# Attention values as one 128-column stationary operand: two passes in place of three, halves added after the product

## The reference, cut to what matters

```
p  = softmax(where(valid, q·k * 64**-0.5 + bias, NEG))      # A, band of 8 chunks
o  = p · v                                                   # einsum 'bhqk,bkhd->bqhd'
mo = softmax(mq · mk * 64**-0.5) · mv                        # M, 4 heads of 64
y  = concat(o, mo) * silu(gate);   x = x + y @ w_out
```

## Time and profile before

| what | value |
|---|---|
| median of three runs | 3016.96 us (3013.03 to 3020.06) |
| span of the profiled execution, first to last instruction | 3014.2 us |
| PE busy | 2789.5 us, 93% |
| PE weight loads busy | 2612.1 us, 87% |
| VectorE busy | 1302.0 us, 43% |
| ScalarE busy | 1317.1 us, 44% |
| GpSimd busy | 684.1 us, 23% |
| mean granted TensorE clock | 0.955 |

### The profile page before, as it was taken

How to read it: one execution, slowest core, us unless ns; L and a number is a source line. 1 busy time by engine, 2 the same in 40 slices (tenths; PEclk the granted TensorE clock), 3 DMA queues, 4 the chain that set the end, 5 groups by cost and what they waited for, 6 DMA issues and landing times.

```text
span 3014.2 us, 46630 instructions
## 1 busy us (share of the span) xinstructions
PE 2789.5 (93%) x18936; PEld 2612.1 (87%) x18936; DVE 1302.0 (43%) x3216; ACT 1317.1 (44%) x2826; POOL 684.1 (23%) x384
## 2 busy tenths in 40 slices
PE   7989999989989999989997988888899989999987
PEld 6979999979989999979987877777699979999887
DVE  4045555552235556652225244444523055555542
ACT  4244544433244555542333355555523245444431
POOL 0212222215121212206211132222142212221212
PEclk9989999999989999989997999999999989999998
DMA  4111111133111112123111000000042111111121
GB/s 148 50 32 56 59 51 48 53 117 99 51 46 50 61 50 71 50 116 100 64 43 32 34 12 10 10 10 3 29 172 73 43 35 64 45 59 45 42 79 65
DMA packets 58197, 171.59 MB, mean 57 GB/s; under 512 B 6720, under 2 KB 15040, under 8 KB 57472
## 3 DMA queue, kind: packets, MB, share of 16 engines
q1 hardware_dynamic: 57984, 168.62, 16.4%
HBM read 134.67 MB, written 33.92 MB: 56 GB/s over the span
## 4 chain that ended last, share of the span: by engine, by line
PE 80%; ACT 9%; DVE 7%; issue 3%; DMA 0%; POOL 0%; SPq 0%; DVEq 0%; ACTq 0%
PE acc L1666 37%; PE acc L1745 10%; PE acc L1618 9%; PE scores L1690 8%; PE turned L1704 6%; PE scores L1576 4%; ACT prob L1147 4%; DVE prob L1407 3%; PE turned L1576 2%; PE scores L1554 1%; DVE pt_split L1436 1%; ACT pt_split L1159 1%; DVE y_sb L1463 1%; ACT prob L1150 1%; PE turned L1716 1%
## 5 line engine op out<-in xcount | busy, mean ns | idle before, releaser
L1666 PE MATMUL acc<-h_split,w_hi 128*128 128x352 f32 (+2 forms) x4860 | 893.2, 330 | 34.1 <-ACT raw L1019 15.3
L1666 PEld LDWEIGHTS acc<-h_split,w_hi 128*128 128x128 f32 x4860 | 790.4, 191 | 62.7 <-ACT raw L1019 19.0
L1490 POOL TENSOR_TENSOR w_lo<-w_raw,w_hi 128x1024 fp32r<-128x1024 f32 (+2 forms) x154 | 333.5, 2168 | 1810.4 <-ACT w_hi L1055 1810.4
L1407 DVE CUSTOM_DVE_ANT_0 prob<-scores,bias 128x256 f32<-128x256 f32 (+9 forms) x576 | 337.6, 633 | 504.7 <-PE scores L1690 501.0
L1436 DVE TENSOR_TENSOR pt_split<-turned,pt_split 128x512 fp32r<-128x512 f32 (+4 forms) x564 | 303.2, 552 | 553.1 <-ACT pt_split L1159 552.6
L1745 PE MATMUL acc<-pt_split,v_split 128*64 128x256 f32 (+6 forms) x3486 | 503.0, 281 | 22.9 <-ACT pt_split L1159 7.3
L1666 PE MATMUL acc<-h_split,w_lo 128*128 128x352 f32 (+2 forms) x2430 | 452.5, 323 | 0.0
L1147 ACT ACTIVATE prob<-prob,stat 128x256 f32<-128x256 f32 (+9 forms) x468 | 303.6, 650 | 329.3 <-DVE stat L1407 329.3
L1745 PEld LDWEIGHTS acc<-pt_split,v_split 128*64 128x64 f32 (+2 forms) x3486 | 405.2, 161 | 40.5 <-issue 14.7
L1666 PEld LDWEIGHTS acc<-h_split,w_lo 128*128 128x128 f32 x2430 | 400.3, 189 | 0.0
L1704 PE MATMUL turned<-ident,prob 128*128 128x128 f32 (+2 forms) x1866 | 290.9, 280 | 96.7 <-DVE prob L1423 51.8
(11 more groups left out here) (129 smaller groups left out, 2785.0 us busy)
## 6 DMA issues: line engine op xcount, KB each, us to landing
w_raw<-w SPq DMA_DIRECT2D x132, 512.0 KB, 3.7
x_scr<-y_sb SPq DMA_DIRECT2D x24, 528.0 KB, 5.5
y_sb<-x_scr SPq DMA_DIRECT2D x24, 528.0 KB, 8.0
y_sb<-x_in SPq DMA_DIRECT2D x16, 528.0 KB, 10.9
mw_raw<-w SPq DMA_DIRECT2D x16, 512.0 KB, 7.6
bias<-rel_in SPq DMA_DIRECT2D x24, 320.0 KB, 4.1
raw<-kcache SPq DMA_DIRECT2D x18, 256.0 KB, 4.0
v_cache<-vcache SPq DMA_DIRECT2D x18, 256.0 KB, 4.0
```

The lines of the kernel that those rows point to most:

```text
L1407: dve.tensor_tensor_reduce(out=prob[0:tile.rows, at:at + tile.width], in0=s_ps[lane][0:tile.rows, tile.at:tile.at + tile.width], in1=bias[ ...
L1490: pool.tensor_tensor(w_lo[:, n % 2, 0:wide], w_raw[:, n % 2, 0:wide], w_hi[:, n % 2, 0:wide].bitcast(F32), ALU.subtract).then_inc(wlo_made ...
L1666: ins = pe.matmul(acc[s.bank][:, 0:s.cols], w[ws][:, 128 * k:128 * k + 128], x(xs, k), start=k == 0 and y == 0, stop=k == s.k_tiles - 1 an ...
```

## The change

For A and M, the values of one block and lane are laid out as four quarters of 64 columns: high of lane 0, low of lane 0, low of lane 1, high of lane 1. The stationary operand is the 128 columns of a lane, high and low together, and there are two passes, with the high and the low half of the probabilities; the low pass waits for `turned_lo` as before, but it now stands behind the first of two passes. For lane 0 the product with the high values is on rows 0 to 63 of `acc[0]` and that with the low values on rows 64 to 127; for lane 1 it is the other way round.

The evacuation becomes: ScalarE copies the rows with the low products into a new SBUF tile `o_low` (two copies of 64 rows, lying where `recip` is), VectorE adds the other rows of `acc[0]` to it (two instructions), waits for that, and multiplies the whole 128 rows into the gate (one instruction, whose end is `o_read`). `acc[0]` is free after the additions (`o_added`). Kinds B and C keep their passes. GpSimd's writing of the ones moves from the start of layer 2 to behind its last M unit.

```diff
+    o_low = sbuf("o_low", [256], at=place[0] - 1024)
+    v_quarters = v_flat[:, 13 * 128:].rearrange("p (b q d) -> p b q d", q=4, d=64)
...
+        if kind == "C":
+            return v_hi[0:rows, block:block + n, :, 0:64], v_lo[0:rows, block:block + n]
+        return v_quarters[0:rows, block:block + n, 0:4:3], v_quarters[0:rows, block:block + n, 1:3]
...
+            elif name == "evac" and item[1].job.kind in "AM":
+                u = item[1]
+                act.wait_ge(*pv_done.upto(u.chunks[-1].p))
+                if u.before is not None:
+                    act.wait_ge(*o_read.upto(u.before.n))
+                act.activation(o_low[0:64, 0:u.qn], acc[0][64:128, 0:u.qn], ACT.Copy).then_inc(o_low_read.mark(u.n), 1)
+                act.activation(o_low[64:128, 0:u.qn], acc[0][0:64, 256:256 + u.qn], ACT.Copy).then_inc(
+                    o_low_read.mark(u.n), 1)
...
+                else:
+                    gate = y_sb[:, u.job.tile, q]
+                    dve.wait_ge(*o_low_read.upto(u.n))
+                    for lane in range(2):
+                        rows = slice(64 * lane, 64 * lane + 64)
+                        ins = dve.tensor_tensor(o_low[rows, 0:u.qn], acc[0][rows, 256 * lane:256 * lane + u.qn],
+                                                o_low[rows, 0:u.qn], ALU.add)
+                    ins.then_inc(o_added.mark(u.n), 1)
+                    dve.wait_ge(*o_added.upto(u.n))
+                    dve.tensor_tensor(gate, gate, o_low[:, 0:u.qn], ALU.mult).then_inc(o_read.mark(u.n), 1)
...
-                elif what == "operands" and more["kind"] == "C":
-                    pool.wait_ge(*normed_hi.upto(norm_key, KT - 1))
-                    pool.wait_ge(*memkv_stored.upto(more["layer"]))
+                elif what == "latents":
+                    pool.wait_ge(*pv_done.upto(more["before"]["unit"].chunks[-1].p))
                     pool.memset(v_hi[:, :, :, 64:128].bitcast(F32), 1.0).then_inc(ones_set.mark("values"), 1)
...
-                pe.wait_ge(*(o_gated if held.job.kind == "C" else o_read).upto(held.n))
+                pe.wait_ge(*(dict(A=o_added, M=o_added, B=o_read, C=o_gated)[held.job.kind]).upto(held.n))
...
-                for y, (vs, ps) in enumerate(PV_PASSES):
-                    if y == 2:
+                passes = PV_PASSES if job.kind in "BC" else ((0, 0), (0, 1))
+                for y, (vs, ps) in enumerate(passes):
+                    if ps == 1:
                         pe.wait_ge(*turned_lo.upto(chunk.a))
...
-                        elif vs == 0 and job.kind == "C":
+                        elif vs == 0:
                             rows, values = 128, v_hi[0:n, block, lane, :]
-                        elif vs == 0:
-                            rows, values = 64, v_hi[0:n, block, lane, 0:64]
```

More of the change, by code:

```diff
@@ L715, in halves_of_v @@
             return [split_v(v_flat[0:rows, 128 * (13 * x + block):128 * (13 * x + block + n)]) for x in range(2)]
-        return v_hi[0:rows, block:block + n, :, 0:64], v_lo[0:rows, block:block + n]
+        if kind == "C":
+            return v_hi[0:rows, block:block + n, :, 0:64], v_lo[0:rows, block:block + n]
+        return v_quarters[0:rows, block:block + n, 0:4:3], v_quarters[0:rows, block:block + n, 1:3]
     pairs = lambda x: x.rearrange("p (a b) -> p a b", a=2)
@@ L748, in encoder @@
     pv_done, o_gated, o_read = signal("pv_done"), signal("o_gated"), signal("o_read")
+    o_low_read, o_added = signal("o_low_read"), signal("o_added")
     scores_ready, scores_biased = signal("scores_ready"), signal("scores_biased")
@@ L1455, in vector_program @@
                                              op0=ALU.mult, op1=ALU.mult).then_inc(o_read.mark(u.n), 1)
-                else:
-                    if u.job.kind == "C":
-                        dve.wait_ge(*sums_logged.upto(u.n))
-                    else:
-                        dve.wait_ge(*pv_done.upto(u.chunks[-1].p))
+                elif u.job.kind == "C":
+                    dve.wait_ge(*sums_logged.upto(u.n))
                     for lane in range(2):
@@ L1463, in vector_program @@
                         ins = dve.tensor_tensor(gate, acc[0][0:64, 256 * lane:256 * lane + u.qn], gate, ALU.mult)
-                    ins.then_inc((o_gated if u.job.kind == "C" else o_read).mark(u.n), 1)
+                    ins.then_inc(o_gated.mark(u.n), 1)
+                else:
[8 more added lines that the diff above has]
+                    dve.tensor_tensor(gate, gate, o_low[:, 0:u.qn], ALU.mult).then_inc(o_read.mark(u.n), 1)
             elif name == "emul" and item[1].job.kind == "C":
@@ L1747, in tensor_program @@
                                         start=c == 0 and i == 0 and y == 0,
-                                        stop=last and i == len(chunk.mults) - 1 and y == 2)
+                                        stop=last and i == len(chunk.mults) - 1 and y == len(passes) - 1)
                 ins.then_inc(pv_done.mark(chunk.p), 1)
```

## The result

The changed kernel takes 3093.05 us (median of 4 runs, 3086.49 to 3097.75), the kernel before 3018.51 us beside it: ratio 1.0249, 95% interval 1.0228 to 1.0269. The direction was forecast, the size was not: +15 us stands in the prediction, +74.5 us came. TensorE executes 18224 matmuls where it executed 18936, 712 fewer, as forecast.

What follows compares the result with a forecast made beforehand. PE, 80% of the chain, bounds some units; the path from last value product to next probabilities bounds others. Terms 5.9 + 3.4 + 3.3 + 2.5 = +15.1 us give a span of 3029.3, so 3032 us; range 3010 to 3046.

Steps and rivals of the forecast that it cites:

- Which units count: PE's time counts in some units; in g4 and M units with one projection, last value product to next probabilities.
- The covered evacuation, +0.6: Where the unit's first turn is a full chunk, the copies run almost beneath DVE's subtraction: +0.6 us.
- g3's stall: In g3 of an A job PE waits 1.0 to 1.1 us for the low half, against 1.05 saved: sum 0.
- The saving of the passes: A chunk of 256 columns goes from six to four matmuls and saves a third, 0.26 us.
- no change: Chunks of 128 columns: eight wide matmuls take 0.72 us or up to 0.9, against 0.86 for twelve narrow.
- The decoded product, +0.3: With 32 columns, twenty wide matmuls replace 30 narrow ones: +0.3 us, ends 0 and +0.6.
- The last A jobs, +1.7 each: Last A job of layers 0 and 3, almost no projections, PE waits for DVE in each unit: +3.4 us together.
- the M jobs: Layers 0, 1 and 3: +1.1 us a layer, +3.3; layer 2, nothing beside its second job: +2.5 us.
- the multiplication at 0.42 us: In the new evacuation, one DVE multiplication of 128 x 256 in SBUF, priced at 0.42 us.
- Rival 3: Slower still: idle PE before g1's decoded product makes the clock fall more often, +6 to +10, 3040 us; chance 0.2.
- Rival 1: Faster: DVE and ACT, busy half of each unit, absorb the new steps, deciding at g2 and g3: 2989 us; chance 0.13.
- The ones on GpSimd, nothing: The 1.49 us of writing ones, now waiting for the last M product, delays nothing; 1.5 us once if uncovered.

Runs made afterwards that it cites:

- e2: The changed kernel with the evacuation of before, reading the high product only, low rows left out: 3013.8 us, ratio 0.9991 to the kernel before.
- e9: The changed kernel with eight matmuls, whose results are overwritten, filling the 1.27 us pause in g4: 3079.1 us, ratio 1.0215 to the kernel before.
- e6: The changed kernel with additions and multiplication behind the next unit's scores, in single-chunk units (g4) behind the normalisation too: 3016.7 us, ratio 0.9999 to before.
- e5: The kernel before with its evacuation moved behind the next unit's score instructions on DVE: 3027.6 us, ratio 1.0046.
- e7: The kernel before with its evacuation behind the next unit's scores, in single-chunk units (g4) behind the normalisation too: 3022.6 us, ratio 1.0030.
- e12: e6 with decoded units narrow and evacuated as before, plus overwritten matmuls in pauses of the last A job and M jobs: 3008.9 us, ratio 0.9986 to before.
- e11: e2 with the second pass given twice, six wide matmuls per chunk in place of four: 3083.0 us, ratio 1.0226 to the kernel before.

## Why the prediction was right and wrong, point by point

**Which units count: right.** g4 was forecast at 8.2 us with 1.1 idle and is 8.55 with 1.27. Its idle time ends with the normalised probabilities, as said.

**The covered evacuation, +0.6:** right in kind. The M units with one projection are 8.03 us instead of 7.27, +0.76. g3's stall was forecast at 1.0 to 1.1 us and is 0.75:

```profile
386.50 0.51 PE L1764 MATMUL acc<-pt_split,v_split 128*128 128x256 f32 x2 [0.75 <-DVE pt_split L1450]
```

**The saving of the passes: too large by a third or more.** The chunk's four matmuls were forecast at 0.52 us and take 0.58 here. PE's busy time in g3, with four chunks, fell from 14.30 to 13.70 us in e2, 0.15 us a chunk, not 0.26. Part of the saving comes back behind the chunk. Before, in g0:

```profile
364.39 0.94 PE L1745 MATMUL acc<-pt_split,v_split 128*64 128x256 f32 x6
365.17 2.70 PE L1666 MATMUL acc<-h_split,w_hi 128*128 128x352 f32 x16
367.71 1.43 PE L1666 MATMUL acc<-h_split,w_lo 128*128 128x352 f32 x8
368.98 0.49 PE L1704 MATMUL turned<-ident,prob 128*128 128x128 f32 x3
```

After, the same chunk:

```profile
373.41 0.72 PE L1764 MATMUL acc<-pt_split,v_split 128*128 128x256 f32 x4
373.99 2.85 PE L1686 MATMUL acc<-h_split,w_hi 128*128 128x352 f32 x16
376.68 1.46 PE L1686 MATMUL acc<-h_split,w_lo 128*128 128x352 f32 x8
377.98 0.49 PE L1724 MATMUL turned<-ident,prob 128*128 128x128 f32 x3
```

The products give 0.78 - 0.58 = 0.20 us, and the 16 matmuls behind them take 2.69 instead of 2.54. Sixteen such matmuls elsewhere in the same g0 take 2.69 before as well (355.03 to 357.72), so it is the run behind six narrow matmuls that was short. Why is not shown. With this, and with +0.11 to +0.18 for each chunk of 128 columns, for which "no change" stood, g0 is +0.12 instead of -0.25, g2 +0.29 and g3 +0.36 instead of 0. An A job at full clock is then 68.9 us (with e9's g1) against 66.9, +2.0 where +0.65 was forecast: some 13 us of the miss over ten jobs. The term failed in pricing 128 columns by the transposition row, 90 ns, instead of the wide rows of B, 150 ns, which stood nearer to the truth of 122 to 130.

**The decoded product, +0.3: right at full clock.** Twenty took 2.61 us in e2, +0.23. In the last A jobs the same twenty took 4.7 us in low clock, 1.4 and 0.95 us more than thirty narrow ones before.

**The last A jobs, +1.7 each, and the M jobs: too small.** With their g4 the last A jobs cost 8.5 and 4.9 us; of the 6.9 and 3.8 us ahead of g4, 4.9 and 3.4 may be clock. Layer 2's M jobs were forecast at +2.5 and cost 7.0. M's layers 0, 1 and 3 were forecast at +1.1 each and cost 2.6 to 4.2. Part of that is a term that I took as fixed, the multiplication at 0.42 us. In the last unit of the second M job it runs beside GpSimd's split of the keys:

```profile
253.70 2.47 POOL L1538 TENSOR_TENSOR k_split<-raw,k_split 128x1056 fp32r<-128x1056 f32 x1
254.35 0.86 DVE L1481 TENSOR_TENSOR o_low<-acc,o_low 64x256 f32<-64x256 f32 x2 [0.58 <-ACT o_low L1220]
255.24 1.20 DVE L1485 TENSOR_TENSOR y_sb<-y_sb,o_low 128x256 f32<-128x256 f32 x1
```

That unit is 9.78 us against 7.86, +1.9 for +1.0. The same holds in all 29 places of the changed kernel where this multiplication overlaps a GpSimd tensor_tensor: it ends 0.2 to 0.3 us after it. Mostly that makes it 0.47 us long, in five units of M jobs 0.93 to 1.20.

**The clock: the step that failed.** Rival 3 had the mechanism, its place and its sign (a pause right before the decoded product) and was given a chance of 0.2 and +6 to +10 us. Lost time rose by 53 us at most. I had counted only more falls at the one depth that the trace showed, 1.4 us. The falls also became deeper, 2.9 us, in six of the eight steady g1 (clock 0.83), and low clock grew in the last A jobs (0.88 to 0.80) and in layer 2's M jobs (0.77 to 0.70) as well, where I had counted none or few. The range ended at 3046 us, and even rival 3's +10 us stayed at 3042. So the forecast's sum put the clock at nothing. Of the 63 us by which the span missed the forecast (78.0 less 15.1), the ten A jobs hold 34 (40.1 for 5.9): some 13 are the products and waits above, the rest, 21, is about what their clock can have cost.

**Rival 1, the evacuation hides:** e2, without the copies and the separate multiplication, is near that case, and it gives -1.6 us, not -27. At full clock the passes save 20 us, and the clock takes up to 18.

**The ones on GpSimd, nothing: right.** They are written from 1669.71 us on, 1.48 us long, and GpSimd's next instruction, at 1686.83, waits for ScalarE's half of the weights, not for them. From layer 2's first projection to its first C job it takes 123.71 us against 123.52.

Of the +75 us, worked out from the spans: the chain +35 at full clock and the passes -20, with about +10 more where both meet, are the work (+25 in the table); the clock is the rest, 53 us at most. 10 to 14 us of it come back when the one pause is filled (e9), part of which is the filling's own. That the chain's place is the cause of the whole loss is shown by e6; open stays how the low clock outside g1 divides between chain and wide products, and why wide products lower it.

## What to carry to other kernels

An evacuation that grows by a microsecond belongs behind the instructions that the next matmuls wait for; here the place of two additions and a multiplication in DVE's order was worth 76 us of 3093, and their existence nearly nothing (e6 is 3 us above e2). The order is no gain by itself: the short evacuation of before, moved to the same places, made its kernel 0.3 to 0.5% slower (e5, e7). Pack two halves into one stationary operand only where enough moving columns follow each load (256 here; at 128 and 32 the wide load costs more than the pass it saves). Price a new pause on TensorE ahead of a stretch of small matmuls twice: once as idle time, once as clock. Low clock where TensorE waits anyway need not be time lost (e12).

## What the hardware showed that I had not expected

- A pause of 1.27 us ahead of a stretch of small wide matmuls went with a clock of 0.83 in most g1, a pause of 0.47 us in a narrow kernel (e5) with full clock in six of eight, and eight matmuls of no use in the 1.27 us gave 14 us back (3093.1 to 3079.1 us).
- With 128 stationary columns the spacing of matmuls is 133, 122 and 131 ns for 256, 128 and 32 moving columns (e11).
- A DVE multiplication with both operands in SBUF took 1.20 us instead of 0.43 beside a GpSimd instruction and ended 0.27 us after it, and so did all 29 that overlapped one, 0.2 to 0.3 us after its end; DVE's additions that read PSUM ran beside the same instruction in their usual 0.86 us.
